# Column groups by branch for the input projection, and x turned before its root is known

## The chip, the core and the metric

The kernel runs on one NeuronCore of a Trainium2 chip. Five engines work side by side and hand over through semaphores: TensorE (PE in the profile; its weight loads are PEld), VectorE (DVE), ScalarE (ACT), GpSimd (POOL) and SyncE (SP, which issues the large loads). The metric is the device time of one execution in microseconds, the median of several runs.

## The reference

It is an encoder trunk of two layers on x of 256 tokens by 1024 features. In each layer:

```
h = rms_norm(x, norm1_g[l])
(aq, ak, av, bq, bk, bv, cq, ck, cv, c_q, c_kv, k_rope) = split(h @ w_in[l])   # 2144 columns
aq, ak = rms_norm per head (64 wide), then axial rotary;  c_q, c_kv = rms_norm, then up-projections
o_a, o_b, o_c, o_d = global, neighbourhood, windowed and latent attention
g = sigmoid(h @ w_gate[l] + b_gate[l]);  y = branch outputs @ w_branch[l]
x = x + sum(g * y) @ w_o[l]
h2 = rms_norm(x, norm2_g[l]);  x = x + square(relu(h2 @ w_ff1[l])) @ w_ff2[l]
```

The output is rms_norm(x, final_g). rms_norm(x, g) is x times a root that belongs to the token, 1 / sqrt(mean of squares + eps), times the gain g of the feature. A root of a token can therefore be applied before a product over the features or after it. The products are done to nearly float32 precision: each operand is split into a high part and a low part (names ending in hi and lo), and each product is three matmuls, high times high, high times low and low times high.

## The kernel before

The 256 tokens are two tiles t of 128. A layer's weights come as a sequence of 64 chunks (CHUNKS): 8 of w_in ("in"), 16 of w_gate with the 4 of w_branch ("y") among them, 4 of w_o, 32 of the MLP. A chunk is two halves. SyncE loads a half into one of RAW = 2 raw buffers as soon as the low split of the half that was there has ended (load_half waits for w_lo_ready). ScalarE makes w_hi from raw (split_hi, L614), VectorE makes w_lo = raw - w_hi (split_lo, L876), both into a ring of four slots, and PE uses them and counts w_used. Everything on an engine runs in the order in which it is written; the table SPLIT_AT (L107) says in which step s of a layer which chunk is split. A step is one chunk.

The input projection has eight chunks of 268 columns. In step s PE multiplies both token tiles with chunk s (project_both, L1469); ScalarE evacuates tile 0 (in_evac, L648), VectorE tile 1 (L1187). Chunk s + 2 is split in step s. In the same steps VectorE takes the squares of A's queries and keys (a_squares at step 2, L924 and L925), multiplies by their roots and gains (a_norm at step 3, L938 and L944) and rotates (a_rotate at step 4, L958 to L965). On VectorE they stand behind the evacuation of the step and ahead of its split. GpSimd makes the roots of A's heads (inverse_root, L513 to L515). Its queue before that is: roots of x; two loads of the gate bias; a wait for w_hi of chunk 3 and small loads; a wait for w_hi of chunk 4 and a load of the bias table (bias_run, L539); then the wait for the squares.

At the start, ScalarE takes the squares of x (square_sum, L624), GpSimd makes the roots (norm, L525 and L526), VectorE scales x to h (L883), and PE turns h block by block (L1311) into four PSUM banks. From there act_hi (ScalarE, L638 and L646) and act_lo (VectorE, L894 and L903) are made, with the gains norm1_g as a scalar per feature. The gains come as rows (vec_rows), which PE turns into columns (L1671) and VectorE copies (vec_all, L1158). Between the layers the same happens at the end of the MLP: mlp_out_last (L1611) has eight pieces of six matmuls, and turn_h stands inside the last piece. x + MLP output is residual, L915.

PE's matmuls of a split product are L1300 to L1302. keep_warm (L1292) is a handful of matmuls on the identity whose results nobody reads. Small jobs of the branches (transposes and small products into bank_x) are set to fixed steps by X_AT; scores, softmax, value products follow from step 8 on. The gates come at step 8 and later; their bias is added by gate_add (L1085).

Of the kernel before, what the change touches and what calls it, by code (L numbers as in the profile page):

```python
# [49 lines left out]
IN_N = 8  # L50
IN_C = IN_W // IN_N
# [17 lines left out]
WMAX = KD * IN_C  # L69
assert NC % RING == 0 and NC % RAW == 0  # L70
# [22 lines left out]
SCORES, SOFTMAX, TURN, VALUES, HEAD_OUT = 8, 9, 10, 11, 12  # L93
# [8 lines left out]
def pairs_at(first, s):  # L102
# [4 lines left out]
SPLIT_AT[0:IN_N + 1] = [[]] + [[s + 2] for s in range(1, IN_N - 1)] + [[IN_N + 1, IN_N + 2], [IN_N + AHEAD]]  # L107
# [29 lines left out]
PIECE_OF_FIRST = [(0, 0, D), (1, 0, D)]  # L137


def pieces(k):  # L140

    return PIECES if k else PIECE_OF_FIRST


def summed_count(k, p):

    return sum(len(pieces(j)) for j in range(k)) + p + 1

# [37 lines left out]
def trunk_kernel(nc, x, norm1_g, w_in, w_gate, b_gate, a_q_norm_g, a_k_norm_g, b_rel_bias, c_sink,  # L186
# [3 lines left out]
    with ctx:  # L190
# [92 lines left out]
        x_landed = [sem(f"x_landed{t}") for t in range(T)]  # L283
        ident_landed = sem("ident_landed")
        cst_landed = sem("cst_landed")
        rows_landed = sem("rows_landed")
        d_rows_landed = sem("d_rows_landed")
# [90 lines left out]
        def chunk_cols(c):  # L378
            return WMAX if CHUNKS[c][0] == "in" else 2048

        def in_bank(j, t, l):

            return j if l and j < 2 else t

        def split_view(buf, c):
            return buf[:, c % RING, 0:chunk_cols(c)]
# [9 lines left out]
        def k_view(buf, c, k):  # L396

            return split_view(buf, c).rearrange("p (k n) -> p k n", k=k)

        def half_view(buf, c, h):  # L400

            n = chunk_cols(c) // 2
            return buf[:, c % RING, h * n:(h + 1) * n]
# [26 lines left out]
        def _(sp):  # L430
            for t in range(T):
                sp.dma_start(xs[:, t, :], x[0, t * P:(t + 1) * P, :]).then_inc(x_landed[t], 16)

            def load_half(c, h, l, g=0):
# [10 lines left out]
                elif kind in ("in", "f1"):  # L445
                    w, n = {"in": (w_in, IN_C), "f1": (w_ff1, 256)}[kind]
                    src = w.rearrange("l (k p) (c n) -> l c p k n", p=P, n=n)[bass.ds(l, 1), bass.ds(i + 2 * g, 1)]
# [20 lines left out]

            for l in range(DEPTH):
                for c in range(MLP_LOOP):  # L470
                    load(c, l)
# [7 lines left out]
            for t in range(T):  # L479
                for m, ready in enumerate((h_ready, h_right_ready)):  # L480
                    sp.wait_ge(ready, T * DEPTH + t + 1)
# [6 lines left out]
        def _(pool):  # L488
# [52 lines left out]
            for l in range(DEPTH):  # L541
                norm(2 * l, l)
                pool.wait_ge(gate_read, l * GATE_N)
                for g in range(2):
                    gate_bias(l, g)
# [22 lines left out]
                pool.dma_start(w_ukv[:, :], d_w_ukv[bass.ds(l, 1)].rearrange("o k n -> (o k) n")).then_inc(lat_landed, 16)  # L568

# [23 lines left out]
        def _(act):  # L593

            act.dma_start(ident, table[:, C_ID:C_ID + P]).then_inc(ident_landed, 16)
            act.wait_ge(rows_clear, 1)
            for v, at, n in ((norm1_g, G1, KD), (norm2_g, G2, KD)):
                rows = vec_rows[DEPTH * at:DEPTH * (at + n), :]
                act.dma_start(rows, v.rearrange("l (k p) -> (l k) p", p=P)).then_inc(rows_landed, 16)

# [9 lines left out]
            def split_hi_half(c, h, l, g=0):  # L610
# [3 lines left out]
                nc.scalar.activation(half_view(w_hi, c, h), raw_half(c, h),  # L614
                                     ACT.Copy).then_inc(w_hi_ready, 1)

            def square_sum(k, p):

                t, a, b = pieces(k)[p]
                if k == 0:  # L620
                    act.wait_ge(x_landed[t], 16)
# [5 lines left out]
            def scale_right(k, t):  # L627

# [145 lines left out]
            for l in range(DEPTH):  # L774
# [11 lines left out]
                for s in range(STEPS):  # L786
# [8 lines left out]
                    if kind == "in" and j:  # L795
                        in_evac(j, l)
# [933 lines left out]
```

## Time and profile before

| | us |
|---|---|
| median of 3 runs | 823.1 (822.63 to 823.55) |
| the profiled execution | 823.43 |
| its span, first to last instruction | 821.6 |
| PE busy | 809.4 |
| DVE, ACT, POOL busy | 565.8, 427.6, 55.9 |

The page of the profile gives the busy time of each engine and a chain, which is followed back from the last instruction to whatever released each step. The timeline lists instructions with their start. A matmul's duration includes time in which the next one already runs, so the distance between two starts is what one of them costs.

### The profile page before, as it was taken

The page shows a single profiled execution, that of the slowest core. Times are in us where ns is not written, and L with a number is a line of the kernel's source. Part 1 is how long each engine was busy: PE and PEld are TensorE (multiplying, and loading weights), DVE is VectorE, ACT ScalarE, POOL GpSimd, SP SyncE. Part 2 cuts the span into 40 slices and gives each one's busy share as a digit, 9 for nine tenths or more (in the row PEclk, how much of TensorE's full clock was granted, in tenths as well). Part 3 has the DMA queues.
Part 4 walks back from the last instruction along what each step waited for, and adds up shares of the span by engine and source line. Part 5 has one row for each costly group of instructions (what it writes and reads, how often), then busy time and mean ns, then how long its engine had stood idle before and what let it go on. Part 6 is the DMA issues. An engine that isn't in the chain of part 4 may idle for free.

```text
span 821.6 us, 12232 instructions
## 1 busy us (share of the span) xinstructions
PE 809.4 (99%) x4451; PEld 680.6 (83%) x4451; DVE 565.8 (69%) x827; ACT 427.6 (52%) x722; POOL 55.9 (7%) x97
## 2 busy tenths in 40 slices
PE   7999999999999999999999999999999999999996
PEld 7997767877898888888899877677778988888885
DVE  6667767867676766666767677688775676666773
ACT  6455765664354444433564476558544554433442
POOL 2430000000010000000013100000000100000000
PEclk9999999999999999999999999999999999999999
DMA  8976653554357555666556757345344575666541
GB/s 278 228 235 203 182 180 105 143 175 161 110 158 231 171 181 181 202 204 203 173 154 194 243 170 209 101 152 162 109 158 147 182 226 183 204 204 192 179 140 51
DMA packets 85658, 145.12 MB, mean 177 GB/s; under 512 B 5036, under 2 KB 54448, under 8 KB 85616
## 3 DMA queue, kind: packets, MB, share of 16 engines
q1 hardware_dynamic: 82912, 137.12, 52.0%
q0 software_dynamic: 2496, 7.36, 3.4%
q8 instruction: 26, 0.43, 0.2%
q14 instruction: 16, 0.13, 0.1%
q10 hardware_dynamic: 208, 0.08, 0.0%
HBM read 143.49 MB, written 1.05 MB: 176 GB/s over the span
## 4 chain that ended last, share of the span: by engine, by line
PE 94%; DVE 3%; ACT 1%; POOL 1%; DMA 0%; issue 0%; POOLq 0%; ACTq 0%
PE bank_w L1300 14%; PE bank_w L1302 13%; PE bank_w L1301 13%; PE bank_acc L1300 8%; PE bank_acc L1301 8%; PE bank_acc L1302 8%; PE bank_w L1595 5%; PE bank_ox L1595 5%; PE bank_w L1597 3%; PE bank_ox L1597 3%; PE bank_acc L1396 2%; PE bank_ox L1426 2%; PE bank_acc L1409 2%; DVE w_lo L876 2%; DMA cst<-in_table 0%; PE bank_ox L1302 0%
## 5 line engine op out<-in xcount | busy, mean ns | idle before, releaser
L876 DVE TENSOR_TENSOR w_lo<-raw,w_hi 128x1024 fp32r<-128x1024 f32 (+1 forms) x256 | 307.6, 1243 | 56.2 <-ACT w_hi L614 55.8
L614 ACT ACTIVATE w_hi<-raw 128x1024 fp32r<-128x1024 f32 (+1 forms) x256 | 259.5, 1061 | 35.7 <-DMA raw<-in_w_gate 11.9
L1300 PE MATMUL bank_w<-w_hi,act_both 128*128 128x268 f32 (+1 forms) x512 | 178.1, 348 | 0.7 <-DVE act_both L903 0.6
L1302 PE MATMUL bank_w<-w_hi,act_both 128*128 128x268 f32 (+1 forms) x512 | 173.9, 340 | 0.0
L1301 PE MATMUL bank_w<-w_lo,act_both 128*128 128x268 f32 (+1 forms) x512 | 173.7, 339 | 0.0
L1300 PEld LDWEIGHTS bank_w<-w_hi,act_both 128*128 128x128 f32 x512 | 96.2, 188 | 16.8 <-issue 6.0
L1302 PEld LDWEIGHTS bank_w<-w_hi,act_both 128*128 128x128 f32 x512 | 96.2, 188 | 11.1
L1301 PEld LDWEIGHTS bank_w<-w_lo,act_both 128*128 128x128 f32 x512 | 96.3, 188 | 10.2 <-issue 0.5
L1300 PE MATMUL bank_acc<-w_hi,part_hi 128*128 128x512 f32 x256 | 100.2, 391 | 0.0
L1301 PE MATMUL bank_acc<-w_lo,part_hi 128*128 128x512 f32 x256 | 100.1, 391 | 0.0
L1302 PE MATMUL bank_acc<-w_hi,part_lo 128*128 128x512 f32 x256 | 99.9, 390 | 0.0
L1595 PE MATMUL bank_ox<-act_both,w_hi 128*128 128x512 f32 x192 | 67.8, 394 | 0.0
L1595 PE MATMUL bank_w<-act_both,w_hi 128*128 128x512 f32 x192 | 67.8, 394 | 0.0
L1302 PEld LDWEIGHTS bank_acc<-w_hi,part_lo 128*128 128x128 f32 x256 | 48.1, 188 | 10.4
L1300 PEld LDWEIGHTS bank_acc<-w_hi,part_hi 128*128 128x128 f32 x256 | 48.1, 188 | 10.2
L1301 PEld LDWEIGHTS bank_acc<-w_lo,part_hi 128*128 128x128 f32 x256 | 48.2, 188 | 8.9
L1597 PE MATMUL bank_w<-act_both,w_lo 128*128 128x256 f32 x192 | 54.1, 282 | 0.0
L1597 PE MATMUL bank_ox<-act_both,w_lo 128*128 128x256 f32 x192 | 54.1, 282 | 0.0
L761 ACT ACTIVATE big<-bank_w 128x512 f32<-128x512 f32 x12 | 7.2, 598 | 74.0 <-PE bank_w L1597 74.0
L761 ACT ACTIVATE big<-bank_ox 128x512 f32<-128x512 f32 x12 | 7.2, 598 | 71.9 <-PE bank_ox L1597 71.9
L1595 PEld LDWEIGHTS bank_ox<-act_both,w_hi 128*128 128x128 f32 x192 | 36.1, 188 | 8.3
L1595 PEld LDWEIGHTS bank_w<-act_both,w_hi 128*128 128x128 f32 x192 | 36.0, 188 | 8.4
(197 smaller groups left out, 1173.8 us busy)
## 6 DMA issues: line engine op xcount, KB each, us to landing
raw<-in_w_ff SPq DMA_DIRECT2D x128, 512.0 KB, 4.6
raw<-in_w_gate SPq DMA_DIRECT2D x64, 512.0 KB, 4.7
raw<-in_w_in SPq DMA_DIRECT2D x32, 536.0 KB, 5.5
raw<-in_w_o SPq DMA_DIRECT2D x16, 512.0 KB, 4.6
gate_row<-in_b_gate POOLq DMA_DIRECT2D x16, 256.0 KB, 4.4
raw<-in_w_branch SPq DMA_DIRECT2D x16, 256.0 KB, 4.5
raw<-in_w_branch SPq DMA_DIRECT2D x8, 512.0 KB, 4.5
xs<-in_x SPq DMA_DIRECT2D x2, 512.0 KB, 4.2
```

The lines of the kernel that those rows point to most:

```text
L614: nc.scalar.activation(half_view(w_hi, c, h), raw_half(c, h), ACT.Copy).then_inc(w_hi_ready, 1)
L761: nc.scalar.activation(side[b].rearrange("p (d s) -> p d s", d=2), wide_banks(i)[:, 0:2, SEQ:2 * SEQ], ACT.Copy).then_inc(u_copied, 1)
L876: nc.vector.tensor_tensor(half_view(w_lo, c, hf), raw_half(c, hf), f32(half_view(w_hi, c, hf)), ALU.subtract).then_inc(w_lo_ready, 1)
L1300: nc.tensor.matmul(dst, s_hi, m_hi, start=first, stop=False)
L1301: nc.tensor.matmul(dst, s_hi, m_lo, start=False, stop=False)
L1302: ins = nc.tensor.matmul(dst, s_lo, m_hi, start=False, stop=last)
L1396: ins = nc.tensor.matmul(bank_acc[:, half, keys], q[:, t * P:(t + 1) * P], k, start=True, stop=True)
L1409: ins = nc.tensor.transpose(bank_acc[:, 2 + b, at:at + P], prob[:, b, t, kt * P:(kt + 1) * P], ident)
L1426: ins = nc.tensor.matmul(bank_o[half * HD:(half + 1) * HD, blk * SEQ:(blk + 1) * SEQ], v, probT[:, half, kt, :], start=(kt == 0), stop=(kt ...
L1595: nc.tensor.matmul(bank, hi[:, kc, f], act_both[:, kc, :, :].rearrange("p m s -> p (m s)"), start=kc == 0, stop=False)
L1597: ins = nc.tensor.matmul(bank[:, 0:SEQ], lo[:, kc, f], act_both[:, kc, 0, :], start=False, stop=kc == KD - 1)
```

## The change

The projection is cut at branch boundaries into five groups (IN_AT) of 512, 384, 384, 512 and 352 columns. A group is two chunks, one for each half of the 1024 features, so there are ten "in" chunks and ten steps; step s is token tile s % 2 of group s // 2, over both of the group's chunks. All later steps move by two. a_squares, a_norm and a_rotate stay at steps 2, 3 and 4. Since a layer now has 66 chunks, the slot in the ring depends on the layer too. h is gone: PE turns raw x, and the root of the token is applied at the evacuation of each group and in gate_add. x is loaded in four blocks of 256 columns, each ahead of a half chunk. In layer 0, group 0 is done block by block: four products with w_hi and act_hi, four with w_hi and act_lo, the turn of the next block, four with w_lo. The loads of the gate bias move down in GpSimd's queue.

```diff
+IN_AT = [AQ, BQ, (BQ + CQ) // 2, CQ, DCQ, IN_W]
+IN_G = len(IN_AT) - 1
+IN_N = 2 * IN_G
...
-SPLIT_AT[0:IN_N + 1] = [[]] + [[s + 2] for s in range(1, IN_N - 1)] + [[IN_N + 1, IN_N + 2], [IN_N + AHEAD]]
+SPLIT_AT[0:IN_N + 1] = [[3], []] + [[s + 2] for s in range(2, IN_N - 1)] + [[IN_N + 1, IN_N + 2], [IN_N + AHEAD]]
...
+            for q in range(4):
+                load_x(q)
+                load_half(q // 2, q % 2, 0)
...
                 norm(2 * l, l)
-                pool.wait_ge(gate_read, l * GATE_N)
-                for g in range(2):
-                    gate_bias(l, g)
...
+            def in_evac(g, l):
+
+                act.wait_ge(in_half, l * IN_G + (g + 1))
+                if g == 0:
+                    act.wait_ge(rstd_ready, 2 * l * T + 1)
+                nc.scalar.activation(qkv[:, 0, IN_AT[g]:IN_AT[g + 1]], in_bank(g, 0, l),
+                                     ACT.Copy, scale=rstd[:, 0:1]).then_inc(in_act, 1)
...
-            square_sum(0, 0)
-            square_sum(0, 1)
-            split_hi_half(0, 0, 0)
             act.wait_ge(vec_ready, 1)
-            turned_hi_both(0, G1, 0, range(0, KD // 2))
-            split_hi_half(0, 1, 0)
-            turned_hi_both(0, G1, 0, range(KD // 2, KD))
-            split_hi(1, 0)
-            in_evac(0, 0)
+            for kc in range(0, KD, 2):
+                turned_hi_first((kc, kc + 1))
+                split_hi_half(kc // 4, kc // 2 % 2, 0)
             split_hi(2, 0)
+            split_hi(3, 0)
+            for p in range(len(PIECES_OF_FIRST)):
+                square_sum(0, p)
...
-                nc.vector.tensor_tensor(gate_slot(g // 2, 2 * t + g % 2), bank_w[:, t, :], gate_row[:, g % 2, :],
-                                        ALU.add).then_inc(gate_read, 1)
+                nc.vector.scalar_tensor_tensor(out=gate_slot(g // 2, 2 * t + g % 2), in0=bank_w[:, t, :],
+                                               scalar=rstd[:, t:t + 1], in1=gate_row[:, g % 2, :], op0=ALU.mult,
+                                               op1=ALU.add).then_inc(gate_read, 1)
...
-                    if kind == "in":
+                    if kind == "in" and j % 2:
                         dve.wait_ge(w_used, used_count(l, j))
...
                     split_lo(0, l + 1)
-                    split_lo(1, l + 1)
                     residual(k, 0, last)
+                    split_lo_half(1, 0, l + 1)
                     residual(k, 1, last)
-                    scale_left(k, 0)
+                    split_lo_half(1, 1, l + 1)
...
+                for kc in range(0, KD, 2):
...
+                    pe.wait_ge(w_hi_ready, kc // 2 + 1)
+                    pe.wait_ge(h_hi_ready, 2 * (kc + 2))
...
+                    if kc < KD - 2:
+                        turn_first(kc // 2 + 1)
+                    pe.wait_ge(w_lo_ready, kc // 2 + 1 + 2 * RAW)
...
+            def project(g, t, l):
+
+                if l or g > 1:
+                    pe.wait_ge((in_act, in_dve)[t], l * IN_G + g)
+                for half in range(2):
+                    if t == 0:
+                        pe.wait_ge(w_lo_ready, lo_count(l, 2 * g + half))
+                    project_part(g, t, l, half)
...
                 part(a, 2)
+                if l + 1 < DEPTH:
+                    turn_x(2 * l + 2, 0)
                 part(a, 3).then_inc(w_used, 1)
+                if l + 1 < DEPTH:
+                    turn_x(2 * l + 2, 1)
                 part(b, 2).then_inc(acc_done, 1)
...
-                    turn_h(l + 1, 0)
```

What VectorE does in steps 2 to 4 of layer 0, before: the evacuation of chunk 2, the split of chunk 4, the evacuation of chunk 3, a_norm, the split of chunk 5 (mix holds A's queries and keys).

```order
L1187 COPY qkv<-bank_w 128x268 [waits w_used]
L876 TENSOR_TENSOR w_lo<-raw,w_hi 128x1072 [waits w_hi_ready] x2
L1187 COPY qkv<-bank_w 128x268 [waits w_used]
L938 TENSOR_TENSOR mix<-qkv,rs_a 128x128 [waits in_dve,gains_landed,rs_a_ready]
L938 TENSOR_TENSOR mix<-qkv,rs_a 128x128 x5
L944 TENSOR_TENSOR mix<-mix,gain_qk 128x256 [waits dve_link]
...
L876 TENSOR_TENSOR w_lo<-raw,w_hi 128x1072 [waits w_hi_ready,dve_link]
```

The same place after: the split of chunk 4, the evacuation of group 1, a_norm, the split of chunk 5.

```order
L896 TENSOR_TENSOR w_lo<-raw,w_hi 128x768 [waits w_hi_ready] x2
L1201 TENSOR_SCALAR qkv<-bank_w,rstd 128x384 [waits w_used]
L948 TENSOR_TENSOR mix<-qkv,rs_a 128x128 [waits in_dve,gains_landed,rs_a_ready]
L948 TENSOR_TENSOR mix<-qkv,rs_a 128x128 x5
L954 TENSOR_TENSOR mix<-mix,gain_qk 128x256 [waits dve_link]
...
L896 TENSOR_TENSOR w_lo<-raw,w_hi 128x768 [waits w_hi_ready,dve_link]
```

a_norm kept its place in the row; the evacuation ahead of it now stands for a whole group, and the split behind it is the second half of the next group.

PE at the start of the program, before: identity matmuls, turns of h, the gain rows, the second tile's turns.

```order
L1292 MATMUL bank_w<-cst 128x128 x4
L1311 MATMUL bank_ox<-cst,big 128x128 [waits h_ready]
L1311 MATMUL bank_acc<-cst,big 128x128 [waits h_right_ready]
L1671 MATMUL bank_acc<-cst,vec_rows 128x38 [waits d_rows_landed,rows_landed]
```

And after: the first block of raw x, the gain rows, identity matmuls, then products, turns of the next block, and products with the low weights.

```order
L1325 MATMUL bank_ox<-cst,xs 128x128 [waits x_landed0,ident_landed]
L1695 MATMUL bank_acc<-cst,vec_rows 128x16 [waits rows_landed]
L1306 MATMUL bank_w<-cst 128x128 x4
L1466 MATMUL bank_acc<-w_hi,act_both 128x512 [waits h_hi_ready,w_hi_ready]
L1470 MATMUL bank_acc<-w_hi,act_both 128x512 [waits h_lo_ready]
L1325 MATMUL bank_ox<-cst,xs 128x128 [waits x_landed1]
L1476 MATMUL bank_acc<-w_lo,act_both 128x512 [waits w_lo_ready]
```

The turns of blocks 1 to 3 moved from ahead of all products to between them.

## Rows read from the trace of the kernel before

**Rows 1.** The page: busy times, the clock in 40 slices, the chain's shares.
```profile
PE 809.4 (99%) x4451; PEld 680.6 (83%) x4451; DVE 565.8 (69%) x827; ACT 427.6 (52%) x722; POOL 55.9 (7%) x97
PEclk9999999999999999999999999999999999999999
PE 94%; DVE 3%; ACT 1%; POOL 1%; DMA 0%; issue 0%; POOLq 0%; ACTq 0%
```

**Rows 2.** Timeline of PE from the start: start us, us, engine, line, what, count.
```profile
4.71 2.50 PE L1292 MATMUL bank_w<-cst 128*128 128x128 f32 x10 [4.71 <-DMA cst<-in_table]
7.13 1.11 PE L1311 MATMUL bank_ox<-cst,big 128*128 128x128 f32 x4
...
9.93 0.60 PE L1311 MATMUL bank_acc<-cst,big 128*128 128x128 f32 x4
```

**Rows 3.** Timeline of PE at the edges of its long stretches.
```profile
11.59 0.36 PE L1300 MATMUL bank_w<-w_hi,act_both 128*128 128x268 f32 x1 [0.61 <-DVE act_both L903]
...
47.28 0.60 PE L1357 MATMUL bank_ox<-cst,qkv 128*128 128x128 f32 x4
...
60.14 0.48 PE L1300 MATMUL bank_w<-w_hi,act_both 128*128 128x512 f32 x1
...
211.86 0.48 PE L1300 MATMUL bank_acc<-w_hi,act_both 128*128 128x512 f32 x1
...
223.02 0.60 PE L1311 MATMUL bank_ox<-cst,xs 128*128 128x128 f32 x4
...
400.87 0.40 PE L1300 MATMUL bank_acc<-w_hi,part_hi 128*128 128x512 f32 x1
...
411.02 0.40 PE L1302 MATMUL bank_acc<-w_hi,part_lo 128*128 128x512 f32 x1
411.79 0.66 PE L1311 MATMUL bank_ox<-cst,big 128*128 128x128 f32 x4 [0.38 <-DVE big L883]
...
463.27 0.48 PE L1300 MATMUL bank_w<-w_hi,act_both 128*128 128x512 f32 x1
```

**Rows 4.** Loads, KB and median us to landing; ScalarE's first evacuations (timeline).
```profile
raw<-in_w_in SPq DMA_DIRECT2D x32, 536.0 KB, 5.5
...
cst<-in_table POOLq DMA_DIRECT2D x1, 480.0 KB, 3.7
vec_rows<-in_norm_g ACTq DMA_DIRECT2D x2, 8.0 KB, 4.5
...
9.99 1.57 ACT L646 ACTIVATE act_both<-bank_ox,vec_all 128x256 fp32r<-128x256 f32 x4 [1.14 <-PE bank_ox L1311]
```

**Rows 5.** Timeline of VectorE in layer 1, steps 2 and 3.
```profile
430.25 0.95 DVE L925 TENSOR_REDUCE ss_a<-mix 128x12 f32<-128x768 f32 x1
...
438.42 0.44 DVE L1187 COPY qkv<-bank_w 128x268 f32<-128x268 f32 x1 [3.03 <-PE bank_w L1302]
438.77 1.29 DVE L938 TENSOR_TENSOR mix<-qkv,rs_a 128x128 f32<-128x128 f32 x6
...
441.29 2.46 DVE L876 TENSOR_TENSOR w_lo<-raw,w_hi 128x1072 fp32r<-128x1072 f32 x2
```

**Rows 6.** Timeline of GpSimd in layer 1, the roots of A's heads.
```profile
432.18 0.63 POOL L539 DMA_DIRECT2D tmp<-in_b_rel_bias  x1 [5.41 <-ACT w_hi L614]
432.82 0.22 POOL L513 TENSOR_TENSOR ss_a<-ss_a,inv_head 128x12 f32<-128x12 f32 x1
...
434.33 3.22 POOL L515 TENSOR_TENSOR rs_a<-ss_a,neg_half 128x12 f32<-128x12 f32 x1
```

**Rows 7.** Timeline of ScalarE in layer 1, step 2: the evacuation and the high split.
```profile
429.51 0.40 ACT L651 ACTIVATE qkv<-bank_w 128x268 f32<-128x268 f32 x1 [4.63 <-PE bank_w L1302]
429.80 2.08 ACT L614 ACTIVATE w_hi<-raw 128x1072 fp32r<-128x1072 f32 x2
```

**Rows 8.** Groups by line and shape: busy us, mean ns, idle time before.
```profile
L1085 DVE TENSOR_TENSOR big<-bank_w,gate_row 128x512 f32<-128x512 f32 x32 | 21.9, 684 | 5.6 <-PE bank_w L1302 5.6
...
L1099 DVE SCALAR_TENSOR_TENSOR mix<-big,bank_w 128x512 f32<-128x512 f32 x8 | 5.5, 688 | 9.8 <-PE bank_w L1302 9.8
```

More of the change, by code:

```diff
@@ L68 @@
 AHEAD = 3
-WMAX = KD * IN_C
-assert NC % RING == 0 and NC % RAW == 0
+WMAX = 2048
+assert NC % RAW == 0
 MLP_LOOP = POS["f1", 1]
@@ L282, in trunk_kernel @@
         w_used = sem("w_used")
-        x_landed = [sem(f"x_landed{t}") for t in range(T)]
+        x_landed = [sem(f"x_landed{q}") for q in range(4)]
         ident_landed = sem("ident_landed")
@@ L568, in _ @@
                 pool.dma_start(w_ukv[:, :], d_w_ukv[bass.ds(l, 1)].rearrange("o k n -> (o k) n")).then_inc(lat_landed, 16)
+                pool.wait_ge(gate_read, l * GATE_N)
+                for g in range(2):
+                    gate_bias(l, g)
                 pool.wait_ge(cst_landed, 16)
@@ L620, in square_sum @@
                 if k == 0:
-                    act.wait_ge(x_landed[t], 16)
+                    for q in range(4):
+                        act.wait_ge(x_landed[q], 16)
                 else:
@@ L794, in _ @@
                         exps(i, l)
-                    if kind == "in" and j:
-                        in_evac(j, l)
+                    if kind == "in" and j and j % 2 == 0:
+                        in_evac(j // 2, l)
                     if kind == "y":
@@ new lines, in project_first_layer @@
+            def project_first_layer():
+                for kc in range(0, KD, 2):
+                    half, k = divmod(kc, KD // 2)
+                    hi, lo = k_view(w_hi, half, KD // 2, 0), k_view(w_lo, half, KD // 2, 0)
+                    toks = [slice(t * P, (t + 1) * P) for t in range(T)]
+                    pairs = [(t, u) for t in range(T) for u in range(2)]
+                    pe.wait_ge(w_hi_ready, kc // 2 + 1)
+                    pe.wait_ge(h_hi_ready, 2 * (kc + 2))
+                    for t, u in pairs:
+                        nc.tensor.matmul(in_bank(0, t, 0), act_hi[:, kc + u, toks[t]], hi[:, k + u, :],
+                                         start=kc + u == 0, stop=False)
+                    pe.wait_ge(h_lo_ready, 2 * (kc + 2))
+                    for t, u in pairs:
+                        nc.tensor.matmul(in_bank(0, t, 0), act_lo[:, kc + u, toks[t]], hi[:, k + u, :],
+                                         start=False, stop=False)
+                    if kc < KD - 2:
+                        turn_first(kc // 2 + 1)
+                    pe.wait_ge(w_lo_ready, kc // 2 + 1 + 2 * RAW)
+                    for t, u in pairs:
+                        ins = nc.tensor.matmul(in_bank(0, t, 0), act_hi[:, kc + u, toks[t]], lo[:, k + u, :],
+                                               start=False, stop=kc + u == KD - 1)
+                        if kc == KD - 2 and (t, u) == (0, 1):
+                            ins.then_inc(in_half, 1)
+                    if k:
+                        ins.then_inc(w_used, 1)
@@ L1551, in last_branch, with token_sum @@
                 turn_mix(1, l)
-            def token_sum(c, a_hi, a_lo, p, start, stop, ks=(0, 1)):
-                hi, lo = k_view(w_hi, c, 2), k_view(w_lo, c, 2)
+            def token_sum(c, l, a_hi, a_lo, p, start, stop, ks=(0, 1)):
+                hi, lo = k_view(w_hi, c, 2, l), k_view(w_lo, c, 2, l)
                 t, a, b = p
```

290 lines of the change are left out of this document (134 added, 156 removed), and 6 rows, old and new, of the table X_AT.

## The prediction

> **What bounds the kernel now.** I read the page from the top down. TensorE (PE) is busy 99% of the span and makes up 94% of the chain that ended last [rows 1]. A busy share hides small gaps, because matmuls overlap, so the spacing of starts is the better measure. In the timeline the first product starts at 11.59 and the transposes of the first small job at 47.28, with 288 products of 268 columns between them: 0.1239 us each. A stretch of 48 products of 512 columns runs from 211.86 to 223.02: 0.2325 us each [rows 3]. Both stretches have no holes. So before the change PE waits almost only at the start (11.6 us) and once at the change of layers (411.02 to 411.79, where 0.23 would do) [rows 3]. A kernel like this gets faster by fewer or cheaper PE instructions or by an earlier start, and slower as soon as the split weights (w_hi from ScalarE, w_lo from VectorE) come late. The question of this change is therefore lateness: in each place, what is queued ahead of the split that PE needs next.
>
> **Products.** Both kernels stream 48 x 2144 columns per layer. Before, that is 384 products of 268; after, 96 of 512, 96 of 384 and 48 of 352. For 384 and 352 no spacing is shown; on the straight line between 268 and 512 they cost 0.1755 and 0.1613 us. Sum: 96 x 0.2325 + 96 x 0.1755 + 48 x 0.1613 = 46.9 us, against 47.7 (60.14 - 11.59 less 0.86 of transposes). That saves 0.8 us a layer.
> The Trainium skill (TensorE: Matmul & The Clock Gate, Back-to-back issue gap) gives the warm gap as N/2.4 plus 2.5 ns, so 114 and 216 ns; by that the saving would be 144 x 2.5 ns = 0.4 us a layer. The rows show 124 and 232 ns, a larger fixed part, and the sum goes by the rows.
>
> **The start of layer 0.** Removed from it: two squares, the roots on GpSimd and four scalings of VectorE ahead of the first transposes. What is last now is the gain rows: the two small loads are issued from 1.2 on and take 4.5 us to land [rows 4], say 5.5; turning and copying them takes 0.25 + 0.2 + 0.2 with handoffs to 6.3; ScalarE then turns out two blocks of 256 columns (four took 1.57, so 0.8) and splits a half chunk (1.0) [rows 4, 7]: first product at **8.3** instead of 11.59, 3.3 us earlier. Before, all eight blocks were turned ahead of the products; now group 0 goes in four stages that form a ring. PE turns block pair q+1 only after its eight products with w_hi of pair q; ScalarE splits half chunk q+1 only after it has evacuated pair q+1. One round: handoff 0.1, two evacuations 0.85, split 1.0, handoffs 0.15, eight products 1.86, four transposes 0.44, handoff 0.1, in all 4.5 us. PE's own work in a round is 12 x 0.2325 + 0.44 = 3.23 us, so it waits 1.27 us, three times: 3.8 us. The 12 transposes (3 x 0.44 = 1.3 us) are now between the products too. And PE starts slow: the granted clock of the page reads full [rows 1], but four transposes take 1.11 us at 7.1 and 0.60 at 9.9 [rows 2], the 1.2 and the 2.4 GHz level. In the kernel before this ended ahead of the first product; now I let three products fall into it, 3 x 0.2 = 0.6 us.
>
> **Chunk 3 of layer 0.** Its second half can be loaded only when the low split of chunk 1's second half has freed the raw buffer. By the rounds above that is at 23.5. A load with an idle queue takes 3.7 us (the table load), the weight loads 5.5 at the median [rows 4]; I take 3.7, since nothing stands before it, and keep 5.5 for the range. Landing 27.3, high split 0.75 and low split 0.87: 29.2. PE needs it at 27.4: a wait of **1.8 us** (3.6 at the other end).
>
> **The step that decides: group 2, both layers.** In the kernel before, chunk s+2 is split in step s, and a step is a whole chunk; the chunk split behind a_norm in step 3 is wanted two steps later. Now a step is one token tile of a group and needs both chunks of the group: chunk 5, split behind a_norm in step 3, is wanted in the middle of step 4. Count from E, the end of group 1's first token tile. PE: second tile 24 x 0.1755 = 4.2, half of group 2's first tile 2.1, so it wants chunk 5 at E + 6.3. The other side: the sums drain 0.2; ScalarE's in_evac 0.45 (0.40 for 268 columns), both halves of chunk 4 at 2.08 x 768/1072 = 1.5 [rows 7]; GpSimd stands in front of w_hi of chunk 4, issues bias_run 0.63, and only then makes the roots of A's heads, 4.73 us (432.82 to 437.55) [rows 6]: E + 7.5. VectorE waits for these roots in a_norm, 2.5 us (438.77 to 441.29), and behind it stand both halves of chunk 5, 2.45 x 768/1072 = 1.75 [rows 5]: E + 11.8, with five handoffs of 0.06 E + 12.1. PE waits **5.8 us**, in each layer. Before, the same roots were ready at 437.55, ahead of VectorE's step 3 at 438.42, so nothing shows of this wait. In layer 0 the second root of x comes late as well and costs part of these 5.8 already at chunk 4; it isn't added. Bounds: even with the roots ready in time, a_norm and the split still follow the end of group 1: 0.2 + 0.5 + 2.5 + 1.75 and handoffs 0.15, less the 2.1 of PE, leave 3.0 us; with 1 us more on GpSimd it is 7.
>
> **Small waits of the same kind.** Chunk 7: drain 0.2, evacuation of 384 columns 0.5, two halves of 1024 2.3 and handoffs, 3.1, against 12 x 0.2325 = 2.8: 0.35. Chunk 9: 0.2 + 0.6 + 1.6 + 0.1 against 1.9 and the 0.36 of transposes: 0.3. Chunk 11 has the transposes of bq as cover and comes out even. Per layer 0.7, bounds 0 and 1.5.
>
> **The change of layers.** Scalings and the first root leave the path; raw x is turned between the last products. 48 products of the MLP's last pieces 11.2, four turns 1.75. VectorE now has a half split between the residual sums; the first sum is done at 406.5, when PE reaches the turn at 407.8, so nothing waits. What is gained here is the wait of 0.5 us.
>
> **Costed at nothing.** VectorE's gate_add reads the root as a scalar: an addition from PSUM takes 684 ns, the form with a scalar 688 [rows 8]. The evacuation of group 0 in layer 1 (in_evac(0) stands behind two more splits, to about 423.3) is wanted at 424.8: 1.5 us of cover. GpSimd's gate rows are issued 1.2 us ahead of the bias additions, steps before either is read. The w_in loads become runs of 2, 1.5 and 1.4 KB instead of 1.1 KB. From the gates on, orders and leads are as before.
>
> **The sum.** Layer 0 up to the first gate product (60.14 before [rows 3]): 8.3 + 46.9 + 0.6 + 1.3 + 3.8 + 0.25 (gain rows) + 1.8 + 5.8 + 0.7 + 0.9 (aq, ak, bq) = 70.35, +10.2. Layer 1 from 400.87 to 463.27, 62.4 us before [rows 3]: 11.2 + 1.75 + 46.9 + 5.8 + 0.7 + 0.9 = 67.25, +4.85. In all +15.0 us. The profiled execution took 823.43 us, its span is 821.6, and it lies 0.3 above the median of 823.1; so 823.43 + 15.0 - 0.3 = **838.1 us**.
>
> **Rivals.** (1) GpSimd's chain costs nothing, because the roots come earlier than counted. For it: sums ready at 430.25 + 0.95 and only 4.73 us of work. Against: the order puts bias_run and its wait for chunk 4 ahead. The lower bound of the wait, 3.0 us a layer, would stay: 838.1 - 2 x 2.8 = 832.5. (2) PE stays the bound, as its 99% say, with every split in time: layer 0 58.25, layer 1 60.75, together -3.5, 819.6 us, faster. The place is the queue of VectorE behind each evacuation, the price 3.5 us, and it decides the sign as soon as all waits together stay under 3.5 us. Against: the ring of the four stages alone costs 3.8. (3) The slow clock: if PE with its waits of 1.3 us in 4.5 stays at the lower level through group 0, each of three rounds costs 8 x 0.2 + 0.4 = 2.0 more, the rest of the group 3.5: about 847. For it: at 7.1 PE ran slow although it had been busy for 2.4 us [rows 2]; against: the 0.77 us without a start at 411.02 [rows 3] left no slow products behind. The Trainium skill (the same page, A second HAM failure mode: psum-queue depth-cycling) describes a kernel whose short idle times between groups make the clock swing; by that rule this rival would hold, and no row here has such a pattern to test it. (4) Loads as late as in the slow stretches, 5.5 us and more, at chunks 3 to 5 of layer 0: about 842. That the change does not do what it says I leave out: the order of the instructions shows all of it.
>
> **How the numbers follow.** My forecast has 0.70 (834 to 842), rival 1 0.06, rival 2 0.04, rival 3 0.10, rival 4 0.10. The range 832 to 845 holds the forecast with its bounds and the rivals 1 and 4, and leaves out 2 and 3. A measurement of this kernel can tell about 0.2%, 1.6 us, from no change; faster by more than that has rival 2 and a bit, 0.05, no change 0.02, slower 0.93.
>
> **What would show it.** The first product at 8.3, four stages 4.5 us apart with 1.3 us holes before the high products of each; the first gate product at 70 and the MLP's last pieces to the first gate product in 67 us; in each layer one hole of 5 to 6 us in the middle of group 2, ended by w_lo of chunk 5, with a_norm waiting 2.5 us and more for GpSimd's root; holes of 0.3 us in groups 3 and 4. Wrong would make it: no wait of a_norm, products of 384 columns far off 0.176 us, or four transposes in the first group still at 1.1 us after 12 us.

## The result and the profile after

| | before | after |
|---|---|---|
| median, us | 823.3 (822.6 to 823.7, 6 runs) | 846.8 (842.1 to 852.6, 6 runs) |
| ratio | | 1.029 (1.025 to 1.033) |
| profiled execution, us | 823.43 | 846.97 |
| its span, us | 821.6 | 845.0 |

The changed kernel is 2.9% slower. The forecast was 838.1 with a range of 832 to 845: the sign is right, the loss of 23.5 us is more than the 15.0 worked out, and the time lies above the range. The runs also spread over 10 us, where those of the kernel before spread over 1.

From the page of the changed kernel: busy times, the clock in 40 slices, the chain's shares, and the group of the first matmul of a split product with its idle time.

```profile
PE 815.1 (96%) x4158; PEld 674.3 (80%) x4158; DVE 567.4 (67%) x824; ACT 425.6 (50%) x722; POOL 52.2 (6%) x97
PEclk9989999999999999999999899999999999999999
PE 85%; DVE 7%; ACT 3%; DMA 2%; POOL 2%; issue 1%; POOLq 0%; ACTq 0%; DVEq 0%
L1314 PE MATMUL bank_w<-w_hi,act_both 128*128 128x512 f32 (+2 forms) x400 | 158.8, 397 | 15.0 <-DVE w_lo L896 14.7
```

PE has 293 matmuls fewer than in [rows 1] and is busy 5.7 us longer; the chain goes through DVE for 7% where it was 3%; PE waits 14.7 us for w_lo; and the clock has a dip early in each of the two layers. Fewer instructions that are busy for longer are slower instructions.

The timeline of PE in the changed kernel at the landmarks (start us, us, engine, line, what):

```profile
7.71 2.07 PE L1466 MATMUL bank_acc<-w_hi,act_both 128*128 128x512 f32 x4
9.58 1.91 PE L1470 MATMUL bank_acc<-w_hi,act_both 128*128 128x512 f32 x4
...
42.84 0.69 PE L1314 MATMUL bank_w<-w_hi,act_both 128*128 128x384 f32 x1 [4.40 <-DVE w_lo L896]
...
55.90 0.50 PE L1314 MATMUL bank_w<-w_hi,act_both 128*128 128x512 f32 x1 [0.96 <-DVE w_lo L896]
...
73.28 0.48 PE L1314 MATMUL bank_w<-w_hi,act_both 128*128 128x512 f32 x1
...
413.80 0.40 PE L1314 MATMUL bank_acc<-w_hi,part_hi 128*128 128x512 f32 x1
...
452.22 0.69 PE L1314 MATMUL bank_w<-w_hi,act_both 128*128 128x384 f32 x1 [4.16 <-DVE w_lo L896]
...
467.02 0.79 PE L1314 MATMUL bank_w<-w_hi,act_both 128*128 128x512 f32 x1 [3.99 <-DVE w_lo L896]
...
486.80 0.48 PE L1314 MATMUL bank_w<-w_hi,act_both 128*128 128x512 f32 x1
```

Against [rows 3] the first gate product of layer 0 comes at 73.28 instead of 60.14 (+13.1). Then nothing is lost for 340 us: the last stretch of layer 0 begins at 413.80 instead of 400.87 (+12.9). The first gate product of layer 1 comes at 486.80 instead of 463.27 (+23.5), and the span ends 23.4 later. All of the loss is in the two projections: 13.1 and 10.6 us, where 10.2 and 4.85 were forecast.

Stretches of the changed kernel: from and to, length, busy us (and count) of PE, PEld, DVE, ACT, POOL, then PE's granted clock, DMA share, GB/s:

```profile
38.00:43.00 5.00, 0.60 (x4) 0.28 (x2) 4.51 (x14) 0.00 (x0) 1.21 (x3) 0.92 1.02 266
43.00:48.00 5.00, 5.00 (x16) 5.00 (x17) 2.85 (x7) 0.91 (x2) 0.00 (x0) 0.50 0.82 230
48.00:52.00 4.00, 4.00 (x22) 4.00 (x21) 2.36 (x2) 3.45 (x4) 1.38 (x3) 0.87 0.25 51
...
448.00:452.00 4.00, 0.06 (x1) 0.00 (x0) 3.93 (x12) 0.00 (x0) 0.72 (x2) 0.97 0.94 194
452.00:455.00 3.00, 2.78 (x9) 2.78 (x10) 2.93 (x8) 0.00 (x0) 0.00 (x0) 0.50 0.89 288
...
462.80:467.00 4.20, 0.23 (x2) 0.00 (x0) 4.17 (x1) 0.00 (x0) 3.07 (x4) 0.81 0.91 324
467.00:472.00 5.00, 4.98 (x12) 3.92 (x13) 0.00 (x0) 0.00 (x0) 0.00 (x0) 0.50 0.27 78
```

Here is what the forecast lacked. PE stands still for over 4 us at 38, 448 and 463; by the clock shares of these rows its clock falls from 2.4 to 1.2 GHz (0.50) in the last 0.4 to 1.6 us of each hole, and the products behind the hole run at half speed, 0.32 us apart instead of 0.176 for 384 columns. PE counts as busy there, which is why it is busier with less to do. Taking each start-to-start distance less the normal one, the half-speed stretches cost 2.9, 1.4 and 2.5 us, 6.8 together. The third hole, at chunk 7 of layer 1, was not in the forecast either. Its cause is in two rows of the timeline, of VectorE and of GpSimd:

```profile
460.66 6.30 DVE L896 TENSOR_TENSOR w_lo<-raw,w_hi 128x1024 fp32r<-128x1024 f32 x2
...
462.28 3.59 POOL L597 TENSOR_TENSOR bias<-tmp,cst 128x384 f32<-128x384 f32 x4
```

Two low splits take 2.4 us elsewhere; these took 6.30. The second began at 461.8, and GpSimd's four bias additions at 462.28; the split ended only after them, 5.17 us long instead of 1.22. The kernel before has the same thing, unseen because PE was not yet in want of that chunk:

```profile
451.80 5.02 DVE L876 TENSOR_TENSOR w_lo<-raw,w_hi 128x1072 fp32r<-128x1072 f32 x1
...
452.05 3.63 POOL L575 TENSOR_TENSOR bias<-tmp,cst 128x384 f32<-128x384 f32 x4
```

The Trainium skill (SBUF — State Buffer, "SBUF: two separate sides") says that a VectorE operation with two inputs from SBUF and a GpSimd operation that reads SBUF share a port pair as an exclusive lock: whichever starts first has it for the whole instruction, and the other blocks. The trace agrees that one blocks: when the additions had ended, at 465.87, the split still took 1.10 of its 1.22 us. It goes beyond the page in that the split was held through four instructions. Who came first can't be read from the recorded starts: the split is recorded 0.48 us ahead of the first addition, yet next to nothing of it was done in that time. In layer 0 of the same execution the additions (53.43) fell beside splits in another way: two of them took 1.33 and 1.89 us instead of 0.95, and the split beside them 1.96.

### The profile page after: what moved, and what is told of

Read it like the earlier page. It is cut to its first block, busy times and chain, and to the rows that moved or that the text cites. A ratio compares the mean times of both kernels' runs of the same rounds, so it can differ in the third digit from the quotient of the medians.

```text
span 845.0 us, 11667 instructions
## 1 busy us (share of the span) xinstructions
PE 815.1 (96%) x4158; PEld 674.3 (80%) x4158; DVE 567.4 (67%) x824; ACT 425.6 (50%) x722; POOL 52.2 (6%) x97
## 4 chain that ended last, share of the span: by engine, by line
PE 85%; DVE 7%; ACT 3%; DMA 2%; POOL 2%; issue 1%; POOLq 0%; ACTq 0%; DVEq 0%
PE bank_w L1314 11%; PE bank_w L1315 10%; PE bank_w L1316 10%; PE bank_acc L1314 9%; PE bank_acc L1315 9%; PE bank_acc L1316 9%; PE bank_w L1622 5%; PE bank_ox L1622 5%; DVE w_lo L896 4%; PE bank_ox L1624 3%; PE bank_w L1624 3%; PE bank_ox L1439 2%; PE bank_acc L1409 2%; PE bank_acc L1422 2%; ACT w_hi L636 1%
## 5 line engine op out<-in xcount | busy, mean ns | idle before, releaser
L896 DVE TENSOR_TENSOR w_lo<-raw,w_hi 128x1024 fp32r<-128x1024 f32 (+2 forms) x264 | 309.1, 1212 | 83.9 <-ACT w_hi L636 83.4
L636 ACT ACTIVATE w_hi<-raw 128x1024 fp32r<-128x1024 f32 (+2 forms) x264 | 258.7, 1032 | 24.4 <-DMA raw<-in_w_gate 8.3
L1314 PE MATMUL bank_w<-w_hi,act_both 128*128 128x512 f32 (+2 forms) x400 | 158.8, 397 | 15.0 <-DVE w_lo L896 14.7
L1315 PE MATMUL bank_w<-w_lo,act_both 128*128 128x512 f32 (+2 forms) x400 | 153.1, 383 | 0.0
L1316 PE MATMUL bank_w<-w_hi,act_both 128*128 128x512 f32 (+2 forms) x400 | 153.0, 383 | 0.0
L1314 PEld LDWEIGHTS bank_w<-w_hi,act_both 128*128 128x128 f32 x400 | 77.2, 193 | 35.7 <-DVE w_lo L896 17.4
L1316 PEld LDWEIGHTS bank_w<-w_hi,act_both 128*128 128x128 f32 x400 | 76.9, 192 | 12.7
L1315 PEld LDWEIGHTS bank_w<-w_lo,act_both 128*128 128x128 f32 x400 | 77.2, 193 | 11.5 <-issue 0.5
L1316 PEld LDWEIGHTS bank_acc<-w_hi,part_lo 128*128 128x128 f32 x256 | 48.1, 188 | 10.2
```

Source lines behind the costliest of these rows:

```text
L636: nc.scalar.activation(half_view(w_hi, c, h, l), raw_half(c, h), ACT.Copy).then_inc(w_hi_ready, 1)
L896: nc.vector.tensor_tensor(half_view(w_lo, c, hf, l), raw_half(c, hf), f32(half_view(w_hi, c, hf, l)), ALU.subtract).then_inc(w_lo_ready, 1)
L1314: nc.tensor.matmul(dst, s_hi, m_hi, start=first, stop=False)
L1315: nc.tensor.matmul(dst, s_hi, m_lo, start=False, stop=False)
L1316: ins = nc.tensor.matmul(dst, s_lo, m_hi, start=False, stop=last)
```

## Experiments

The theory after comparing the traces: (a) the hole at chunk 5 is VectorE's order, a_norm ahead of chunk 5's low split; (b) these holes bring the clock down, which costs 1.4 to 2.9 us more behind each; (c) the hole at chunk 7 is GpSimd's additions holding VectorE; (d) the waits of the opening are PE's late turns. The main rival to (b) was that the clock falls for another reason, such as the short waits of the opening.

**e1: chunk 5's low split first.**

```diff
                     if s == 3:
+                        split_lo(5, l)
                         a_norm(l)
...
-                    if kind != "y":
+                    if kind != "y" and s != 3:
```

> The changed kernel with one move on VectorE: the low split of chunk 5 stands ahead of the norm of A's heads instead of behind it. Theory (the order on VectorE makes the 4.7 and 4.5 us waits at chunk 5, and TensorE's clock falls because of them): the wait at chunk 5 shrinks from 4.74 to about 0.5 us in layer 0 and from 4.50 to about 0.8 in layer 1, and the half-speed products behind it (2.7 and 1.3 us of excess) go too. That is some 12 us off 846.8, so 834 to 836, less what comes back as a wait at chunk 7, which TensorE then reaches earlier: up to 3 us. Rival (the clock falls for another reason than this wait): the waits go, and half-speed products of about the same length stay in group 2 or 3: 838 to 840. Rival (the loads are late): chunk 5's split itself comes late and the wait stays above 3 us: 843 or more.

Measured: 829.8 us (828.1 to 830.8), ratio 1.008 (1.006 to 1.010). That is 17.0 us off the changed kernel, more than the 11 to 13 expected. PE in the timeline:

```profile
38.28 0.44 PE L1315 MATMUL bank_w<-w_hi,act_both 128*128 128x384 f32 x1
...
46.53 0.47 PE L1315 MATMUL bank_w<-w_hi,act_both 128*128 128x512 f32 x1 [1.71 <-DVE w_lo L896]
```

Chunk 5 is taken up at 38.28 with 0.1 us lost in layer 0 and 0.5 in layer 1. No half-speed product is left behind the opening. The hole at chunk 7 went as well (0.46 and 0.70 us of excess instead of 1.12 and 4.14): everything in the group shifted, and the additions now come after the split. With the half-speed products behind it that gave 6.6 us, of which 3.6 came back as new waits at chunk 6, 1.88 and 1.70 us; this and a shorter slow start (0.5 us) make most of the 4 us more than expected. (a) holds. That the collision went too was luck: nothing in this edit aimed at it.

**e2: the roots of A's heads first on GpSimd.**

```diff
-                pool.wait_ge(w_hi_ready, hi_count(l, 4, 1))
-                bias_run(l, 0)
                 pool.wait_ge(ss_a_ready, l + 1)
                 inverse_root(rs_a..., ss_a..., inv_head...).then_inc(rs_a_ready, 1)
+                pool.wait_ge(w_hi_ready, hi_count(l, 4, 1))
+                bias_run(l, 0)
```

> The changed kernel with one move on GpSimd: the roots of A's heads stand ahead of the first of the two bias loads and its wait for chunk 4's high split. Theory (the norm on VectorE waits for the roots, and the load is in the roots' way): the roots end 0.66 us earlier in layer 0 and 3.7 us earlier in layer 1, where VectorE takes the norm up as soon as its evacuation is done, 1.17 us earlier. The wait at chunk 5 falls to about 4.1 and 3.3 us, in all 1.9 us off; with it the half-speed stretches get shorter or go: 840 to 845. Rival (the roots do not matter, the norm's 2.5 us and the split's 1.8 us are the whole): nothing, 846 to 847.

Measured: 847.1 us, runs from 839.3 to 850.4: no difference that this spread lets one see. In layer 1 the wait at chunk 5 fell to 3.07 us of excess, near the 3.3 worked out, and PE ran at half speed for 11 products behind it all the same. In layer 0 it stayed at 4.6, where 4.1 was expected. GpSimd there:

```profile
34.48 0.85 POOL L535 TENSOR_TENSOR ss_a<-ss_a,inv_head 128x12 f32<-128x12 f32 x1 [0.79 <-DVE ss_a L936]
35.41 0.81 POOL L536 TENSOR_TENSOR ss_a<-ss_a,eps 128x12 f32<-128x12 f32 x1
```

The bias load no longer stood in front, but these two small operations now fell beside chunk 4's low split (34.31 to 36.15) and took 0.85 and 0.81 us; in layer 1, with no split beside them, they took 0.20 and 0.21. At chunk 7 the profiled execution has holes in both layers, 4.15 us in layer 1 and a new one of 4.18 us in layer 0, whose two rows are:

```profile
51.52 6.30 DVE L897 TENSOR_TENSOR w_lo<-raw,w_hi 128x1024 fp32r<-128x1024 f32 x2
...
53.15 3.59 POOL L598 TENSOR_TENSOR bias<-tmp,cst 128x384 f32<-128x384 f32 x4
```

So the collision is not tied to layer 1. Where the small gain of this edit went is read from this one execution; across runs it is not shown.

**e3: the bias additions after chunk 7's low split.**

```diff
                 pool.wait_ge(bias_landed, l * 32 + 32)
+                pool.wait_ge(w_lo_ready, lo_count(l, 7))
```

> The changed kernel with one wait more on GpSimd: its four bias additions start only when chunk 7's low split is done. Theory (VectorE's low split of chunk 7 is held while GpSimd adds; in layer 1 its second half took 5.17 us where one takes 1.21): the two halves take 2.4 us instead of 6.3 in layer 1, and 2.4 instead of 3.1 in layer 0; the wait at chunk 7 in layer 1 falls from 4.38 to about 0.5 us and the half-speed products behind it (2.5 us) go: 6.5 us off, 840. Rival (the split is late because its raw half or its high half is late): the wait stays within 1 us of 4.38, and the time within 1 us of 846.8. Rival (the clock falls there whatever the wait is): 843.

Measured: 839.4 us (838.4 to 839.8), ratio 1.020 (1.018 to 1.022), 7.5 us off. VectorE, GpSimd and PE at the same place:

```profile
459.61 2.35 DVE L897 TENSOR_TENSOR w_lo<-raw,w_hi 128x1024 fp32r<-128x1024 f32 x2
...
462.14 3.63 POOL L598 TENSOR_TENSOR bias<-tmp,cst 128x384 f32<-128x384 f32 x4 [0.94 <-DVE w_lo L897]
...
462.02 0.50 PE L1315 MATMUL bank_w<-w_hi,act_both 128*128 128x512 f32 x1
```

The splits take 2.35 us, PE waits 0.2 us instead of 4.14, and no half-speed product follows there. (c) holds. The spread over its four runs is 1.3 us instead of 10, with chunk 5's holes still there: as far as four runs show, most of the changed kernel's spread hangs on this collision.

**e4: idle time filled with products that are thrown away.** Two runs. The counts shown are those of the second; the first had ((46, 10), (42, 38)), which was the wrong size.

```diff
+            def fill(n):
+                for _ in range(n):
+                    nc.tensor.matmul(bank_o[:, 0:P], ident, ident, start=True, stop=True)
...
                     if t == 0:
+                        if half and g in (2, 3):
+                            fill(((18, 3), (17, 16))[l][g - 2])
                         pe.wait_ge(w_lo_ready, lo_count(l, 2 * g + half))
```

> The changed kernel with idle time of TensorE filled: ahead of the waits at chunks 5 and 7 it multiplies the identity with itself (46 and 10 times in layer 0, 42 and 38 in layer 1, 88 ns each) into a bank that nobody uses, so 4.0, 0.9, 3.7 and 3.3 us of the waits are work that is thrown away. What is computed otherwise is unchanged, and so are all waits. Theory (the idle time makes the clock fall): the waits end when they ended, and the products behind them run at full speed: 2.7, 1.3 and 2.5 us off, 6.5 in all, 840. The spread over runs shrinks from the changed kernel's 10 us to 1 or 2. Rival (the clock falls for another reason, say the pattern of short waits in the opening or the switch of banks): half-speed products stay, and the time stays at 845 to 848.

Measured: 857.1 us (856.0 to 857.6). The price of a fill was wrong: 88 ns is the mean of four transposes of L1325; a product of the identity shows as two records 111 ns apart, 222 ns in all, so 46 of them took 10.2 us and outlasted the wait. One thing it shows all the same: no half-speed product is left behind the fills, and the runs lie within 1.6 us.

> The changed kernel with TensorE's idle time filled, now in the right size: the fills of the run before took 222 ns for each product of the identity with itself and not 88, so they outlasted the waits by 5.6 and 3.0 us and more. Here 18 and 3 of them stand ahead of the waits at chunks 5 and 7 in layer 0, and 17 and 16 in layer 1: 4.0, 0.7, 3.8 and 3.5 us of work that is thrown away. Theory (idle time makes the clock fall): the products behind the waits start when they started in the changed kernel and run at full speed, 2.7, 1.3 and 2.5 us off, 840, and the runs lie within 2 us. Rival (the clock falls for another reason, such as the short waits of the opening): half-speed products stay behind chunk 5, 845 to 848.

Measured: 844.9 us (843.8 to 846.3), 1.9 us off instead of 6.5. PE's fill at chunk 5, and then stretches of this kernel in pairs, the hole and what follows it, at chunk 5 and chunk 7 of layer 0 and chunk 7 of layer 1:

```profile
38.58 4.18 PE L1311 MATMUL bank_ox<-cst 128*128 128x128 f32 x36
43.14 0.44 PE L1319 MATMUL bank_w<-w_hi,act_both 128*128 128x384 f32 x1 [0.38 <-DVE w_lo L896]
```

```profile
38.60:43.10 4.50, 4.16 (x37) 3.96 (x35) 4.31 (x13) 0.00 (x0) 1.08 (x3) 1.00 1.03 272
43.20:49.50 6.30, 6.30 (x36) 6.13 (x36) 5.30 (x9) 3.97 (x5) 1.13 (x2) 1.00 0.73 192
52.40:56.60 4.20, 0.85 (x7) 0.64 (x5) 4.17 (x1) 0.00 (x0) 3.08 (x4) 0.97 0.89 311
56.70:59.70 3.00, 3.00 (x7) 2.40 (x8) 0.00 (x0) 0.00 (x0) 0.00 (x0) 0.50 0.43 122
...
465.00:469.20 4.20, 3.76 (x33) 3.54 (x31) 4.15 (x1) 0.00 (x0) 3.06 (x4) 1.00 0.84 307
469.30:474.00 4.70, 4.70 (x21) 3.87 (x22) 0.32 (x1) 1.72 (x3) 0.00 (x0) 1.00 0.29 79
```

Within one execution this tells the two apart. The filled holes at chunk 5 (shown for layer 0, the same in layer 1) and at chunk 7 of layer 1 last as long as before, and behind them PE stays at 1.00. The hole at chunk 7 of layer 0, which got three fills and turned out 4.2 us long, is followed by 0.50. (b) holds: the idle time brings the clock down, not what went before it, such as the waits of the opening, which are the same here. The time moved little because full speed behind chunk 5 took PE to chunk 7 of layer 0 2.4 us earlier, into the collision, where the changed kernel's own profiled execution waits 1.1 us. The Trainium skill (TensorE: Matmul & The Clock Gate, "HAM oscillation — how this bites in real kernels") describes a kernel in which each wait for the next load lowers the clock, so that each next stretch starts slow. The trace agrees, with 0.50 behind each unfilled hole shown here.

**e5 and e6: the opening, and chunk 6's low split first.** e5 is e1 with the turns of x moved; e6 is e5 with the rotation moved behind chunk 7's low split.

```diff
                 for kc in range(0, KD, 2):
+                    if kc < KD - 2:
+                        turn_first(kc // 2 + 1)
                     pe.wait_ge(w_hi_ready, kc // 2 + 1)
...
-                    if kc < KD - 2:
-                        turn_first(kc // 2 + 1)
```

> The kernel with chunk 5's low split first (829.8), and the opening changed: each quarter of x is turned at the start of the stage before it instead of ahead of that stage's last four products. Theory (in each of the three waits of 1.39 us TensorE waits for the chain that its own late turns start: turn, evacuation, high split): all three waits of 1.17 us of excess go, 3.5 us off: 826.3. Rival (the raw halves of chunk 1 land too late, at 10.6 and 12.7 us): the waits keep half their length, 828. Rival (the gain is given back at chunk 3, whose second raw half is asked for by the low split of chunk 1): chunk 3's wait of 1.17 us grows by what was won, 829 to 830.

Measured: 824.9 us (824.0 to 826.1, 10 runs), ratio 1.002 (1.001 to 1.003), 4.9 us off e1 where 3.5 were expected. PE in the timeline, the first rows of stages 1 to 4:

```profile
8.14 2.06 PE L1469 MATMUL bank_acc<-w_hi,act_both 128*128 128x512 f32 x4
...
12.60 1.18 PE L1469 MATMUL bank_acc<-w_hi,act_both 128*128 128x512 f32 x4
...
15.80 1.17 PE L1469 MATMUL bank_acc<-w_hi,act_both 128*128 128x512 f32 x4
...
18.65 1.07 PE L1469 MATMUL bank_acc<-w_hi,act_both 128*128 128x512 f32 x4
```

From stage 2 to 3 and from 3 to 4 it is now 3.20 and 2.85 us instead of 4.48 and 4.46; none of the three waits is left, and chunk 3's wait fell from 1.17 to 0.52 us. (d) holds, and chunk 3 gave nothing back. The first eight products still fall partly into half speed (1.3 us).

```diff
-                    if s == 4:
-                        a_rotate(l)
...
                                 split_lo(c, l)
+                    if s == 5:
+                        a_rotate(l)
```

> The kernel of the run before it in this list, and the rotation of A's heads moved on VectorE from ahead of chunk 6's low split to behind chunk 7's. Theory (the waits of 1.88 and 1.70 us at chunk 6, which came with chunk 5's split first, are VectorE's again): about 1.0 us off in layer 0, where chunk 6's second high half is late too, and 1.5 us off in layer 1: 823.8, which is the time of the kernel before (822.9) within 0.2%. Rival (chunk 6 is late by its loads, issued behind GpSimd's): nothing, 826.3. Rival (the rotation now meets GpSimd's additions and holds VectorE, so chunk 8's split is late): 828 or more. In none of these is it faster than the kernel before; the sum for no wait at all in the projections is about 820.

Measured: 824.0 us (823.0 to 825.4, 11 runs), ratio 1.0012 (1.0003 to 1.0021). Only 1.0 us off e5, not 2.5; that the time is the expected one (823.8) is luck, since e5 had given 1.4 us more than its forecast. Chunk 6's wait is gone in layer 1 and 0.7 us shorter in layer 0, but chunk 7's grew to 0.92 us in both layers. The rotation met the additions, as the rival said, and one of its four operations was held, 4.4 us instead of 0.35, but nobody wanted it:

```profile
44.54 5.19 DVE L968 TENSOR_TENSOR mix<-mix,cst 128x192 f32<-128x192 f32 x4
```

**e7: waiting for the low split by halves.** On top of e6, PE waits for two of a chunk's four rows of 128 at a time.

```diff
-                    if t == 0:
-                        pe.wait_ge(w_lo_ready, lo_count(l, 2 * g + half))
-                    project_part(g, t, l, half)
+                    for ks in ((0, 1), (2, 3)):
+                        if t == 0:
+                            pe.wait_ge(w_lo_ready, lo_count(l, 2 * g + half) - (ks[0] == 0))
+                        project_part(g, t, l, half, ks)
```

> The kernel with chunk 5's and 6's low splits first and the earlier turns (824.0), and one change on TensorE: from group 1 on it waits for the low split of a chunk by halves, two of its four rows of 128 at a time, instead of for the whole chunk before the first product. Theory (what is left at chunks 3, 4, 6 and 7, 0.47, 0.39, 1.26 and 0.92 us in layer 0 and 0.52 and 0.92 in layer 1, is the second half's split, 0.96 to 1.23 us, that comes while six products of the first half could run): nearly all of these go but about 0.3 us of chunk 6: 3 to 4 us off, 820.5, which would be 0.3% faster than the kernel before. Rival (each wait moves on to the second half, since that is what is late): 1 us off, 823. Rival (a new hole elsewhere, at the gates, since TensorE arrives there earlier): nothing, 824.

Measured: 822.5 us (821.0 to 823.9, 11 runs), ratio 0.9991 (0.9982 to 1.0000): 1.5 us off e6, not the 3 to 4 of the theory but nearer to the first rival, and no different from the kernel before. The waits at chunks 3 and 4 went to 0.3 us or less; of chunk 6 of layer 0 this is left, and 0.91 and 0.48 us at chunk 7:

```profile
39.66 0.47 PE L1315 MATMUL bank_w<-w_hi,act_both 128*128 128x512 f32 x1 [0.77 <-DVE w_lo L896]
```

**e8: the changed kernel once more.**

> The changed kernel as it is, once more, for its spread. Theory (its spread of 10 us is two things that fall out differently from run to run: whether the half-speed stretches cover 8 or 18 products, and whether chunk 7's low split in layer 0 is held by GpSimd's additions, which the profile of the changed kernel shows in layer 1 alone): the profile shows in layer 0 at chunk 7 either a wait of about 4.2 us or one of about 1.1, and half-speed products behind each wait of over 3 us, of a count that differs from 18, 8 and 12; the times lie between 842 and 853. Rival (the spread comes from elsewhere, such as the loads): the waits and the half-speed stretches of the profile repeat to within 0.3 us while its time differs from 847 by over 1 us.

Measured: 847.7 us (844.7 to 849.3). Stretches: behind chunk 5, the hole at chunk 7 and behind it in layer 0; behind chunk 5 and the hole at chunk 7 in layer 1:

```profile
43.60:46.40 2.80, 2.80 (x9) 2.80 (x10) 2.73 (x7) 0.00 (x0) 0.00 (x0) 0.50 0.97 223
...
53.90:58.20 4.30, 0.40 (x2) 0.00 (x0) 4.30 (x1) 0.00 (x0) 3.26 (x4) 0.82 0.89 317
58.30:63.30 5.00, 5.00 (x12) 3.94 (x13) 0.00 (x0) 0.00 (x0) 0.00 (x0) 0.50 0.26 77
...
456.90:462.60 5.70, 5.70 (x18) 5.70 (x19) 2.91 (x7) 1.55 (x3) 0.00 (x0) 0.50 0.54 184
468.40:469.60 1.20, 0.42 (x2) 0.00 (x0) 1.20 (x1) 0.00 (x0) 1.20 (x2) 1.00 0.91 315
```

The same kernel, the other way round, with the same counts of slow products in other places; the rival, that the waits repeat, is out. In layer 0 the slow stretch behind chunk 5 is short (8 products, 1.4 us), and PE comes into the collision: 4.16 us at chunk 7, 12 slow products behind. In layer 1 it is long (18 products, 2.8 us) and the wait at chunk 7 is 1.12 us. In the first profile it was layer 0 that had the long stretch (19) and layer 1 the short one (9). One layer pays about 2.9 + 1.1 us or about 1.4 + 4.1 + 2.5, a difference of 4 us for each layer; two layers would make 8 of the spread of 10. No profile of the changed kernel shows both layers alike; e2's, at 850.4 us, has the collision in both.

## Why the prediction failed

Step by step, each measured on the changed kernel's trace.

- **Products.** Right: 384 columns are 0.1755 us apart at full speed, 352 are 0.161 to 0.162.
- **The first product.** 7.71 instead of 8.3. Right in kind, since the gain rows and the first evacuations set it.
- **The half-speed start.** Mis-sized: all eight products of the first stage fell into it, not three. 1.7 us instead of 0.6.
- **The ring of four stages.** Right: rounds of 4.48 and 4.46 us (forecast 4.5), three waits of 1.16 us and 0.1 at each restart, 3.8 in all.
- **Chunk 3.** 1.3 us instead of 1.8; the load landed as assumed.
- **Group 2.** Right in cause and order, with a_norm waiting 1.87 us for GpSimd's root in layer 0 and 1.17 in layer 1. The rows of VectorE in layer 0:

```profile
38.42 1.30 DVE L948 TENSOR_TENSOR mix<-qkv,rs_a 128x128 f32<-128x128 f32 x6 [1.87 <-POOL rs_a L537]
39.76 1.17 DVE L954 TENSOR_TENSOR mix<-mix,gain_qk 128x256 f32<-128x256 f32 x4
40.96 1.83 DVE L896 TENSOR_TENSOR w_lo<-raw,w_hi 128x768 fp32r<-128x768 f32 x2
```

  The size was too large: 4.6 and 4.3 us instead of 5.8, because GpSimd made the roots in 3.6 and 2.9 us (34.77 to 38.39, 444.84 to 447.76), and not in the 4.7 of [rows 6]. Those 4.7 were themselves lengthened beside a split. A row of VectorE before, then one of GpSimd after:

```profile
432.84 2.55 DVE L876 TENSOR_TENSOR w_lo<-raw,w_hi 128x1072 fp32r<-128x1072 f32 x2
...
445.46 2.30 POOL L537 TENSOR_TENSOR rs_a<-ss_a,neg_half 128x12 f32<-128x12 f32 x1
```

  The step that took 3.22 us in [rows 6], beside the second of these two splits, takes 2.30 in both layers of the changed kernel, with no split beside it.
- **What follows the hole.** This is the step that failed. "PE waits 5.8 us, in each layer" was priced as idle time alone. A slow clock was weighed only as rival 3, for the short waits of the opening, where it did not come: the last three stages ran at 1.00. What the runs showed in its place: it came behind the long holes, 1.4 to 2.9 us behind each, 6.8 in all, and went when they were filled (e4) or closed (e1, e3). The argument used against it was a gap of 0.77 us [rows 3], which says nothing on one of four.
- **Small waits.** "Chunk 7: ... 0.35" took two halves of a split at 2.3 us. In layer 1 they took 6.3, and the wait was 4.1 us. The row that warned of it (a low split of 5.02 us beside the additions) was in the trace of the kernel before, ahead of the same step, and was not looked at, since nobody waited for it there.

The sum: 15.0 + 6.8 (clock behind the holes) + 4.6 (chunk 7: 5.3 for 0.7 in the two layers together) + 1.1 (start) - 2.7 (holes at chunk 5) - 1.3 (0.6 of the first product, 0.5 of chunk 3, and 0.2 that is left over) = 23.5, as measured. The time is the one of rival 3, by another mechanism; that rival is wrong.

The remaining question is what the five groups are worth without the holes. e7 still waits about 1 us in places and opens at half speed, and ends level with the kernel before. That the rest could be had too is only argued.

## What to carry to other kernels

Price a hole on TensorE twice: its length, and the half-speed stretch behind it, which here cost 1.4 to 2.9 us for holes of 4.1 to 4.6 and made the time vary from run to run. Waits of 1.7 to 1.9 us (chunk 6 in e1 and e5) had none behind them. When a change shortens the lead between a split and its use, look in the old trace for every instruction of that queue that took several times its usual length, even where nobody waited for it. Before adding work to hide such a wait, first move the one instruction that stands in front of what is wanted: two lines in e1 gave back 17 of 23.5 us, though 6.6 of these came at chunk 7 by luck.

## What the runs showed of the hardware

- When GpSimd's four additions (3.6 us together) meet a VectorE operation of two SBUF inputs, the VectorE operation can be held until all four have ended: 5.02 to 5.20 us instead of 1.22 for the low split, in nine places (one in the kernel before, one after, two each in e2 and both runs of e4, one in e8), and about 4.4 instead of 0.35 for one operation of the rotation, in both layers of e6 and e7. In these the first addition is recorded 0.25 to 0.54 us after the start of the operation that is held. The rotation's would have been over by then, so the recorded starts don't tell who came first.
- In three other places (layer 0 of the kernel before, layer 0 of the changed one, layer 1 of e8) the first addition is recorded 0.68 to 0.76 us after a split's start. That split kept its usual length, the first two additions were stretched to 1.3 and 1.9 us, and the next split to about 2.0.
- GpSimd's small operations on the roots were the ones held when they were recorded 0.17 to 0.28 us after a split's start: 0.8 to 1.1 us instead of 0.2. So what decides who is held is open.
- The clock can fall after work has begun again. In e2, layer 1, PE stood still for 3 us up to 455.15, ran two products at full speed, and was at 0.52 from 455.5 to 459.0.
- The start differs although its code is nearly the same: 8 products at half speed in the changed kernel and e8, 6 in e1 and e3, 5 in e6, 3 in e7 and 1 in the first run of e4.
